# Two projections of the pool moved beside the last pair of heads of an attention, and the pool's chain of steps rewritten

## What is computed

```python
proj = h @ w_in                      # u_pool 512, q, k, v 512 each, g_a, g_b 1024 each
y_a = pool_mixer(u_pool, w_pool, pool_scale)
y_b = stick_breaking_attention(q, k, v)          # 8 heads of 64
merged = sigmoid(g_a) * (y_a @ w_branch_a) + sigmoid(g_b) * (y_b @ w_branch_b)

def pool_mixer(u, w_pool, pool_scale):   # 4 groups of 128 channels, windows 2, 4, 8, 16
    pooled[g] = trailing_mean(u[g], window[g]) - u[g]
    return (pooled[g] @ w_pool[g]) * pool_scale
```

## Time and profile before

| | before |
|---|---|
| median of 3 runs | 2946.78 us (2942.09 to 2948.8) |
| the profiled execution | 2942.8 us, span 2941.0 us |
| busy PE, PEld | 2821.1 us (96%), 2261.9 us (77%) |
| busy DVE, ACT, POOL | 1309.8, 916.1, 802.1 us |
| TensorE's mean granted clock | 0.988 of full speed |

### The profile page before, as it was taken

The page is one execution under the profiler, slowest core; times in us unless marked ns, Lnnn a source line. Parts: engine busy times, 40 slices in busy tenths (PEclk is TensorE's granted clock), DMA queues, the critical chain, the costliest instruction groups (busy, mean ns, idle before and its releaser), DMA issues.

```text
span 2941.0 us, 31529 instructions
## 1 busy us (share of the span) xinstructions
PE 2821.1 (96%) x12846; PEld 2261.9 (77%) x12846; DVE 1309.8 (45%) x1448; ACT 916.1 (31%) x1467; POOL 802.1 (27%) x428
## 2 busy tenths in 40 slices
PE   8999999999999999999999999888999999999996
PEld 6666678887788888888877777677767888888885
DVE  6777642231434434432443545326364343444436
ACT  6666421121311111111254233356352312222223
POOL 2433422223212221222243211123431222121224
PEclk9999999999999999999999999999999999999998
DMA  3000011122123222221112101011321111111113
GB/s 113 22 22 9 22 47 53 48 73 79 71 86 116 93 86 100 95 78 51 57 50 94 60 29 36 29 54 58 115 83 47 50 51 49 44 44 50 51 46 126
DMA packets 60864, 182.90 MB, mean 62 GB/s; under 512 B 6473, under 2 KB 15913, under 8 KB 60593
## 3 DMA queue, kind: packets, MB, share of 16 engines
q1 hardware_dynamic: 60720, 180.89, 17.8%
HBM read 165.61 MB, written 15.25 MB: 61 GB/s over the span
## 4 chain that ended last, share of the span: by engine, by line
PE 82%; DVE 5%; ACT 5%; issue 4%; POOL 2%; DMA 2%; SPq 0%; DVEq 0%; POOLq 0%; ACTq 0%
PE psum_mem L543 65%; PE psum_mem L579 2%; PE psum_mem L837 1%; PE psum_mem L842 1%; PE psum_mem L839 1%; PE psum_mem L614 1%; POOL w_lo L2833 1%; PE psum_mem L617 1%; PE psum_mem L615 1%; PE psum_mem L901 1%; PE psum_mem L1066 1%; PE psum_mem L643 1%; DVE left L2060 1%; PE psum_mem L867 1%; ACT w_hi L1203 1%
## 5 line engine op out<-in xcount | busy, mean ns | idle before, releaser
L2833 POOL TENSOR_TENSOR w_lo<-w_raw,w_hi 128x1024 fp32r<-128x1024 f32 (+1 forms) x233 | 549.0, 2357 | 1795.4 <-ACT w_hi L1203 1795.4
L543 PE MATMUL psum_mem<-h_hi,w_hi 128*128 128x512 f32 x2192 | 685.3, 394 | 23.2 <-DVE h_lo L1944 14.0
L543 PE MATMUL psum_mem<-h_hi,w_lo 128*128 128x512 f32 x2192 | 679.7, 391 | 12.0 <-POOL w_lo L2833 12.0
L543 PE MATMUL psum_mem<-h_lo,w_hi 128*128 128x512 f32 x2192 | 678.2, 391 | 0.0
L543 PEld LDWEIGHTS psum_mem<-h_hi,w_hi 128*128 128x128 f32 x2192 | 412.3, 189 | 115.7 <-issue 25.3
L543 PEld LDWEIGHTS psum_mem<-h_hi,w_lo 128*128 128x128 f32 x2192 | 412.3, 189 | 103.5 <-POOL w_lo L2833 18.0
L543 PEld LDWEIGHTS psum_mem<-h_lo,w_hi 128*128 128x128 f32 x2192 | 413.9, 189 | 87.6
L1203 ACT CAST w_hi<-w_raw 128x1024 fp32r<-128x1024 f32 (+1 forms) x233 | 234.0, 1005 | 658.2 <-PE psum_mem L543 511.4
L1949 DVE TENSOR_TENSOR tmp_mem<-psum_mem,norm_row 128x1024 f32<-128x1024 f32 x46 | 56.2, 1225 | 295.3 <-PE psum_mem L543 295.2
L2266 DVE TENSOR_TENSOR x_block<-x_block,psum_mem 128x1024 f32<-128x1024 f32 x88 | 107.4, 1220 | 67.7 <-PE psum_mem L543 65.1
L2876 POOL TENSOR_TENSOR beta<-beta,left 128x128 f32<-128x128 f32 (+2 forms) x96 | 86.8, 905 | 143.5 <-DVE left L2060 141.5
(11 more groups left out here) (355 smaller groups left out, 4006.7 us busy)
## 6 DMA issues: line engine op xcount, KB each, us to landing
ada_raw<-in_w_ada SPq DMA_DIRECT2D x48, 512.0 KB, 4.5
w_raw<-in_w_up_b SPq DMA_DIRECT2D x44, 512.0 KB, 3.3
w_raw<-in_w_in_a SPq DMA_DIRECT2D x32, 512.0 KB, 3.2
w_raw<-in_w_ffn_gate SPq DMA_DIRECT2D x22, 512.0 KB, 3.6
w_raw<-in_w_ffn_up SPq DMA_DIRECT2D x22, 512.0 KB, 3.6
w_raw<-in_w_ffn_down SPq DMA_DIRECT2D x22, 512.0 KB, 4.7
w_raw<-in_w_down_b SPq DMA_DIRECT2D x22, 512.0 KB, 3.2
w_raw<-in_w_in_b_ml SPq DMA_DIRECT2D x16, 512.0 KB, 4.1
```

Of the source, the lines that this page charges most:

```text
L543: made = e.matmul(pairs.half(use, half), wt, x[:, half_of(half)], start=at == 0 and part == 0, stop=at == len(rhs) - 1 and part == 2, skip ...
L2833: e.tensor_tensor(w_lo[:, i, 0:width], w_raw[:, i, 0:width], w_hi[:, i, 0:width].bitcast(F32), ALU.subtract).then_inc(*S.of("w_lo", c))
```

## The change

In pair 3 the filler becomes `pool_steps`: w_u 0 and w_u 1 are computed there, as 32 groups of three matmuls into banks 6 and 7. It yields twice for each group, so one group is issued in each iteration. ACT copies the first result from PSUM into tmp (`u_raw`) and converts the weights of w_u 1 and w_u 2 within the loop. Behind the attention PE's order is now w_u 2, w_u 3, map 0, map 1, w_ga 0, w_gb 0, map 2, map 3, w_ba 0. A map's result is scaled and rounded by ACT straight from PSUM, and DVE makes ya_lo from PSUM in one instruction; the scaled copy and the subtraction of u become one too. The four yb_lo of POOL stand in a row. The core of the diff (the generators of DVE and POOL that only yield, the names of semaphores, and the drain of the filler behind the loop are left out):

```diff
@@ -210,13 +210,15 @@
             units.append(("w_qkv", io["w_in_a"][4 + 4 * part + j]))
     for g in range(4):
         units.append(("w_u", io["w_in_a"][g]))
-        if g > 0:
-            units.append(("w_pool", io["w_pool"][g - 1]))
     for m in range(KD):
+        if m == 0:
+            for g in (0, 1):
+                units.append(("w_pool", io["w_pool"][g]))
         units.append(("w_ga", io["w_in_a"][16 + m]))
         units.append(("w_gb", io["w_in_a"][24 + m]))
         if m == 0:
-            units.append(("w_pool", io["w_pool"][3]))
+            for g in (2, 3):
+                units.append(("w_pool", io["w_pool"][g]))
         units.append(("w_ba", io["w_branch_a"][m]))
         units.append(("w_bb", io["w_branch_b"][m]))
     for m in range(KD):
...
@@ -625,6 +627,32 @@
                             yield
                             turn_values(j, half)
+            def pool_steps():
+
+                for g in range(2):
+                    n = take("w_u")
+                    i = n % 2
+                    for half in range(NH):
+                        out, cols = bank(6 + half), half_of(half)
+                        if g == 0:
+                            w.wait_ge("v_lo", (3, half, 1))
+                        else:
+                            w.wait_ge("u_raw", half)
+                        w.wait_ge("w_hi", n)
+                        for k in range(KD):
+                            high, low = w_hi[:, i, block_of(k)], w_lo[:, i, block_of(k)]
+                            e.matmul(out, high, h_hi[:, k, cols], start=k == 0, stop=False, skip_group_check=True)
+                            e.matmul(out, high, h_lo[:, k, cols], start=False, stop=False, skip_group_check=True)
+                            w.wait_ge("w_lo", n)
+                            made = e.matmul(out, low, h_hi[:, k, cols], start=False, stop=k == KD - 1,
+                                            skip_group_check=True)
+                            if k == KD - 1:
+                                made.then_inc(*S.of("u_full", (g, half)))
+                                if half == NH - 1:
+                                    unit_end[n] = ("u_full", (g, half))
+                            yield
+                            yield
+
             def score(i):
                 j, par, g, before, n, first, blocks = CHUNKS[i]
                 z = bank(i % 2)[:, 0:blocks * P]
...
@@ -683,10 +711,10 @@
             score(0)
             for i in range(len(CHUNKS) + MIX_AFTER + 4):
                 j, step = divmod(i, PER_PAIR)
-                if step == 0:
+                if step == 0 and j < 4:
                     for _ in filler:
                         pass
-                    filler = qkv_steps(j + 1) if j < 3 else iter(())
+                    filler = qkv_steps(j + 1) if j < 3 else pool_steps()
                 if i + 1 < len(CHUNKS):
                     score(i + 1)
                 next(filler, None)
...
@@ -698,24 +726,29 @@
                         mix(q, b)
                 next(filler, None)
+            for _ in filler:
+                pass
+
             def map_group(g):
                 one("w_pool", ("pool", g), [(pl_hi[g % 2], pl_lo[g % 2], (("pl_hi", g), ("pl_lo", g)))],
-                    (("pooled", g),), (0,))
-
-            pairs.begin(4, [(("beta", LAST),), (("weight_lo", LAST),), (("y", len(SUMS) - 1),), (("v_lo", (3, 1, 1)),)])
-            for g in range(len(WINDOWS)):
+                    (("ya_lo", g),), (0,))
+
+            pairs.begin(4, [(("beta", LAST),), (("weight_lo", LAST),), (("y", len(SUMS) - 1),), (("u", 1),)])
+            for g in (2, 3):
                 one("w_u", ("u", g), h_rhs("a"), (("u", g),))
-                if g > 0:
-                    map_group(g - 1)
             rhs_a = [(ya_hi[:, k, :], ya_lo[:, k, :], (("ya_hi", k), ("ya_lo", k))) for k in range(4)]
             rhs_b = [(yb_hi[:, k, :], yb_lo[:, k, :], (("yb_hi", k), ("yb_lo", k))) for k in range(4)]
             for m in range(KD):
+                if m == 0:
+                    map_group(0)
+                    map_group(1)
                 one("w_ga", ("ga", m), h_rhs("a"), (("g_a", m),))
                 one("w_gb", ("gb", m), h_rhs("a"), (("g_b", m),))
                 if m == 0:
+                    map_group(2)
                     map_group(3)
                 one("w_ba", ("ba", m), rhs_a, (("by_a", m),), range(4))
                 one("w_bb", ("bb", m), rhs_b, (("by_b", m),), range(4))
...
@@ -1283,6 +1316,18 @@
                             yield
                             take_values(j, half)
+            def pool_steps():
+                for g in range(2):
+                    unit()
+                    for half in range(NH):
+                        for k in range(KD):
+                            yield
+                            yield
+                        if g == 0:
+                            w.wait_ge("u_full", (g, half))
+                            w.wait_ge("q_lo", (3, 0, 1))
+                            e.copy(tmp[:, 0, half_of(half)], bank(6 + half)).then_inc(*S.of("u_raw", half))
+
             for par in range(2):
                 cut_q(0, 1, par)
                 cut_k(0, 1, par)
...
+            for _ in filler:
+                pass
+
             for event in at_end["attn"]:
                 w.wait_ge(*event)
-            def map_group(g):
-                unit()
-                w.wait_ge("pooled", g)
-                e.copy(ya_hi[:, g, :], tmp[:, 1, :]).then_inc(*S.of("ya_hi", g))
-
-            for g in range(len(WINDOWS)):
-                unit()
-                for k in ((0, 1), (2, 3), (), ())[g]:
-                    e.copy(yb_hi[:, k, :], yb_raw[:, k, :]).then_inc(*S.of("yb_hi", k))
-                if g > 0:
-                    map_group(g - 1)
+            def mapped(g):
+                w.wait_ge("full", ("pool", g))
+                e.activation(ya_hi[:, g, :], pairs.whole(("pool", g)), ACT.Copy, bias=0.0,
+                             scale=vec("pool_scale", g)).then_inc(*S.of("ya_hi", g))
+
+            def pooled(g):
                 w.wait_ge("u_centred", g)
                 if g >= 2:
                     w.wait_ge("full", ("pool", g - 2))
                 e.copy(pl_hi[g % 2][:, :], tmp[:, 0, :]).then_inc(*S.of("pl_hi", g))
+            def mixed_high(k):
+                e.copy(yb_hi[:, k, :], yb_raw[:, k, :]).then_inc(*S.of("yb_hi", k))
+
+            unit()
+            mixed_high(0)
+            mixed_high(1)
+            pooled(0)
+            mixed_high(2)
+            mixed_high(3)
+            unit()
+            pooled(1)
+            unit()
+            unit()
+            mapped(0)
+            mapped(1)
+            pooled(2)
+            unit()
+            pooled(3)
+            unit()
+            unit()
+            unit()
+            mapped(2)
+            mapped(3)
+
             def merged_to_h(k):
                 w.wait_ge("merged", k)
...
             made.then_inc(*S.of("u_zero", 0))
-            def map_group(g):
-                w.wait_ge("full", ("pool", g))
-                if g > 0:
-                    w.wait_ge("ya_hi", g - 1)
-                    w.own("ya_lo")
-                e.tensor_scalar(tmp[:, 1, :], pairs.whole(("pool", g)), vec("pool_scale", g), None,
-                                ALU.mult).then_inc(*S.of("pooled", g))
-
             def map_low(g):
                 w.wait_ge("ya_hi", g)
                 if g == 0:
                     w.wait_ge("yb_lo", 3)
                     w.wait_ge("yb_hi", 3)
-                e.tensor_tensor(ya_lo[:, g, :], tmp[:, 1, :], ya_hi[:, g, :].bitcast(F32),
-                                ALU.subtract).then_inc(*S.of("ya_lo", g))
+                e.scalar_tensor_tensor(out=ya_lo[:, g, :], in0=pairs.whole(("pool", g)), scalar=vec("pool_scale", g),
+                                       in1=ya_hi[:, g, :].bitcast(F32), op0=ALU.mult,
+                                       op1=ALU.subtract).then_inc(*S.of("ya_lo", g))
             for g, window in enumerate(WINDOWS):
                 u, a, b = u_mem
-                w.wait_ge("full", ("u", g))
-                if g > 0:
-                    w.wait_ge("pl_hi", g - 1)
-                    w.own("pl_lo")
-                unscale(u[:, PAD:], pairs.whole(("u", g))).then_inc(*S.of("u", g))
-                if g > 0:
-                    map_group(g - 1)
+                if g == 0:
+                    w.wait_ge("u_raw", 1)
+                elif g == 1:
+                    w.wait_ge("u_full", (1, 1))
+                else:
+                    w.wait_ge("full", ("u", g))
+                w.own("u_centred")
+                unscale(u[:, PAD:], tmp[:, 0, :] if g == 0 else psum[:, 6:8, :].rearrange("p a b -> p (a b)") if g == 1
+                        else pairs.whole(("u", g))).then_inc(*S.of("u", g))
                 src, dst, width = u, a, 1
                 w.own("u_zero")
                 w.own("u")
@@ -2130,16 +2196,23 @@
```

(41 more changed lines are left out.)

42 lines of the change are left out of this document (26 added, 16 removed).

## The result

The changed kernel takes 2925.57 us, median of 4 runs (2920.84 to 2929.98), beside 2947.79 us (2942.09 to 2949.29, 4 runs) of the kernel before on the same chip: a ratio of 0.9932 [0.992, 0.9944]. The profiled execution took 2928.25 us, with a span of 2926.5, 14.5 less than before.

A forecast was written before the change was run, and what follows sets the result against it. Pair 3 was taken as bound by DVE's scan, not PE's full-clock work; behind it PE is full. 23.5 - 11.1 + 2.0 + 1.0 = 15.4, taken as 15: 2946.8 - 15 = 2932 us, range 2923 to 2941 (own range 2926 to 2937).

The forecast's parts named there:

- the rival of the chain: Pair 3's loop sets the pace, so each iteration grows by 0.80 us; gain about 4, 2943 us; chance 0.13.
- that of a clock at half through most of the pair: Pair 3: PE's clock stays at half through most of it, making the kernel slower, up to 2987 us; chance 0.04.
- unevenness and lag: Pair 3: 1.0 us added for uneven wants of PE and DVE, 1.5 for lag between nearly full engines.
- w_u 0 and 1 gone: Behind the attention: these two units no longer run there, which saves 23.5 us, half clock at their start included.
- The waits behind: From w_u 2 to the first branch: of 5.2 us of waits, 1.2 and 2 stay, 2.0 are won.
- The one at map 1: At map 1: PE waits 2 us, as DVE's group 1, slowed by POOL, comes late by 1 to 2.
- The stall at w_bb 0: At w_bb 0: its stall of 1.01 us goes, since ACT's chain no longer follows map 3; 1.0 won.
- The joined steps: DVE: they save about 0.7 us a group and 1.2 a map, but lie under PE's work, counting for nothing.
- The last rival: At w_gb 0: the pool's chain on DVE is 10 us later than thought, 8 lost, 2939 us; chance 0.07.
- My 2 us of room: At w_gb 0: DVE's taking of w_u 3 from its banks was given 2 us before PE would wait.
- The loss of DVE beside POOL: Behind the attention: with 12 us of POOL's work there, DVE loses about 9 us; by the skill's rule 12.
- The rival of the clock: Pair 3: the clock falls all the same, 13.4 us at half clock lose 6.7; gain 8, 2939 us; chance 0.13.

The follow-up runs named there:

- Two groups everywhere: The changed kernel with two filler groups in every iteration of pair 3, all 32 in the first 16: 2928.82 us, ratio 0.9944 to the kernel before.
- the late filler: The changed kernel with pair 3's filler started 8 iterations later on every engine: 2931.46 us, ratio 0.9954 to the kernel before.
- w_u 0 and 1 behind: The changed kernel with w_u 0 and w_u 1 computed behind the attention's loop, no filler in pair 3: 2936.27 us, ratio 0.9975 to the kernel before.

## Why the prediction was right, point by point

- **What bounds the kernel.** As said: PE full from 291.5 us on, and its work that is moved into idle time is won, up to what then waits for DVE and POOL. Two groups everywhere cost what a fixed amount of work gives, so the rival of the chain (0.13) is out; that of a clock at half through most of the pair (0.04) is too.
- **Pair 3.** The first four iterations grew by 1.6 us (I had 1.0), the next nineteen by 5.9 (I had 7.7 with unevenness and lag), the tail by 2.6 (2.4): 10.2 in all, not 11.1. The last scan came 8.05 us later, w_u 2 at 334.87, as foretold. Of the 2.5 us for unevenness and lag between nearly full engines (lag up to 4.8 in my bounds) 0.7 came; PE never idles from 291.5 to 323.5 us.
- **w_u 0 and 1 gone.** 23.5 us, of which the attention takes 10.2 back: the kernel without the filler measures the difference, with the clock's part in it, at 13.3, of which 0.4 go again in the rest: 12.85.
- **The waits behind.** I took 3.2 us to stay and 2.0 to be won. The one ahead of w_ga 0's low part is 1.46 (I had 1.2). The one at map 1 was mis-sized: 2 us in the sum, none in the run, because pl_lo 1 ended 0.6 us before PE came for it. In its place stand 0.34 us at w_gb 0. So 3.1 us were won. (PE's idle time there fell by only 2.2, from 4.0 to 1.8: by the distance of starts a wait costs about 0.3 us more than its idle time.)
- **The stall at w_bb 0.** The branch lost 1.17 us; I had 1.0.
- **The joined steps.** The step that was wrong: "they lie under PE's work and count for nothing". Apart, the groups' steps cost 2.4 us, in two waits on DVE's chain and the fall of the clock behind the first. The same sentence says that they pay for part of the loss to POOL, and yet the 2 us at map 1 stand in the sum. So two errors on one thing met in it, 2 us of wait put in and the steps that removed it (2.5 us earlier at pl_lo 1) left out. The last rival (0.07) has a right place, w_gb 0: the idle PE there with w_u 3's row as the releaser, which I had named as a sign of being wrong, came with 0.34 us, with 0.78 with two groups in the first four iterations, and with 1.57 with two everywhere. My 2 us of room there were not there.
- **The loss of DVE beside POOL.** Right in size: 2.9 us for two sums, some 8 in all up to pl_lo 1 where I had 9. It cost nothing in the changed kernel, since it lay under PE's work. The Trainium skill ("SBUF — State Buffer", Who interferes with whom) has it that a DVE instruction with two SBUF inputs and a reading GpSimd instruction exclude each other whole. The trace agrees to the smallest shape: a 128x2 patch took 2.24 us beside POOL and ended with POOL's w_lo; the same took 0.16 in the kernel before, with POOL idle. What I drew from it, map 1 later still, did not come about.
- **The rival of the clock** (0.13) was half right, and that was not to be seen in one profile. Six of the profiled executions have one group behind each score at the start of pair 3. In three of them the clock was 1.00 there; in three it fell for a while: 0.79, 0.65 and 0.57 as the mean from 280 to 288 us. The attention took 65.3 us in the first three, and 65.3, 66.7 and 66.6 in the others, so the fall costs up to 1.4 us, not the 6.7 of the rival. In the four with two groups there it stayed at 1.00, and in the three without any (the kernel before, the late filler, w_u 0 and 1 behind) it was 0.50 over the same 8 us. The Trainium skill ("TensorE: Matmul & The Clock Gate", What's actually happening) says that activity releases the throttle; this order agrees with it.

The sum by its terms is 23.53 - 10.16 + 3.14 + 1.17 = 17.68 instead of 15.4. The forecast stood above the time by 6.4 us; 2.3 are these terms, 0.4 the rounding of 15.4 to 15. The terms don't explain the rest, which is of the size of the spread: the medians of one kernel are 2925.57 and 2930.04, and by the second it gains 16.5. The gain by the first medians, 22.2, lies above my 10 to 20; what the clock does elsewhere in an execution stood in no term of mine, so that the time came inside the range is in part luck.
